# Key rows of every other group of four tokens built on ScalarE instead of VectorE, in a hybrid decoder step

## The reference, cut to what matters

```python
    e1 = jnp.take_along_axis(si[:, :, 0], ci // PEER_TOPK, axis=-1)
    e2 = jnp.take_along_axis(si[:, :, 1], ci % PEER_TOPK, axis=-1)
    experts = e1 * N_KEYS + e2
    g = jax.nn.softmax(cv, axis=-1)
    act = jax.nn.gelu(jnp.einsum('nhkd,nd->nhk', expert_u[experts], x).astype(jnp.float32))
    return jnp.einsum('nhk,nhkd->nd', (g * act).astype(x.dtype), expert_v[experts])
```

## Time and profile before

| | us |
|---|---|
| median of 3 runs | 2068.55 (2056.76 to 2073.18) |
| the profiled execution's own time | 2088.97 |
| its span | 2087.2 |
| PE busy | 1867.2 (89%) |
| DVE busy | 1522.3 (73%) |
| POOL busy | 654.2 (31%) |
| ACT busy | 608.7 (29%) |

### The profile page before, as it was taken

How to read it: one execution, slowest core, us unless ns; L and a number is a source line. 1 busy time by engine, 2 the same in 40 slices (tenths; PEclk the granted TensorE clock), 3 DMA queues, 4 the chain that set the end, 5 groups by cost and what they waited for, 6 DMA issues and landing times.

```text
span 2087.2 us, 26461 instructions
## 1 busy us (share of the span) xinstructions
PE 1867.2 (89%) x8833; PEld 1441.2 (69%) x8833; DVE 1522.3 (73%) x3495; ACT 608.7 (29%) x1037; POOL 654.2 (31%) x518
## 2 busy tenths in 40 slices
PE   6999899789997899699579789999999999999995
PEld 3556584366665664466457656888888888888884
DVE  4025238545546664679998878899999999999988
ACT  1133021200110120111245633443334343433343
POOL 0000001155635013414000012455555565566630
PEclk9989999866656558899789899999999999999998
DMA  6600335056647146656145589999999999999991
GB/s 258 234 32 33 112 122 191 15 152 211 223 157 261 56 138 225 242 202 244 59 152 203 230 315 328 333 392 381 388 397 389 379 381 386 398 381 384 383 340 43
DMA packets 157719, 508.71 MB, mean 244 GB/s; under 512 B 15760, under 2 KB 72640, under 8 KB 136128
## 3 DMA queue, kind: packets, MB, share of 16 engines
q1 hardware_dynamic: 90560, 266.44, 34.6%
q0 software_dynamic: 67072, 241.21, 31.1%
HBM read 474.69 MB, written 31.45 MB: 243 GB/s over the span
## 4 chain that ended last, share of the span: by engine, by line
PE 59%; DVE 22%; DMA 7%; issue 7%; ACT 3%; POOL 2%; SPq 0%; DVEq 0%; ACTq 0%
PE ps L1086 13%; PE ps L1070 12%; PE ps L677 5%; PE ps L1016 4%; DVE lo L2156 3%; PE ps L1032 2%; PE ps L825 2%; PE ps L786 2%; PE ps L1057 2%; DMA lo<-ur,lo 2%; PE ps L764 2%; PE ps L846 2%; PE ps L763 2%; PE ps L978 2%; POOL lo L1546 2%
## 5 line engine op out<-in xcount | busy, mean ns | idle before, releaser
L1546 POOL DMA_INDIRECT lo<-ur,lo x224 | 288.4, 1287 | 787.8 <-DVE lo L2093 345.0
L1546 POOL DMA_INDIRECT lo<-vr,lo x224 | 298.8, 1334 | 467.9 <-DVE lo L2164 300.2
L1086 PE MATMUL ps<-vh,hx 128*128 128x512 f32 x768 | 242.3, 397 | 23.6 <-DVE vl L2129 18.7
L1070 PE MATMUL ps<-xh,uh 128*128 128x320 f32 x832 | 257.8, 310 | 0.0
L1070 PE MATMUL ps<-xl,uh 128*128 128x320 f32 x832 | 257.1, 309 | 0.0
L1070 PE MATMUL ps<-xh,ul 128*128 128x320 f32 x832 | 256.8, 309 | 0.0
L1186 ACT ACTIVATE hi<-ps 128x512 f32<-128x512 f32 (+11 forms) x251 | 146.3, 626 | 326.4 <-PE ps L1016 107.7
L1086 PE MATMUL ps<-vl,hx 128*128 128x512 f32 (+1 forms) x768 | 240.4, 395 | 0.0
L2156 DVE SCALAR_TENSOR_TENSOR lo<-lo 128x1024 f32<-128x1024 f32 x168 | 215.4, 1282 | 11.8 <-DVE lo L2156 1.1
L1086 PEld LDWEIGHTS ps<-vh,hx 128*128 128x128 f32 x768 | 139.4, 189 | 60.1 <-issue 32.7
L2129 DVE TENSOR_TENSOR vl<-hi,vh 128x1024 fp32r<-128x1024 f32 x128 | 156.5, 1223 | 31.0 <-ACT vh L1186 14.3
(11 more groups left out here) (406 smaller groups left out, 3079.4 us busy)
## 6 DMA issues: line engine op xcount, KB each, us to landing
hi<-ev SPq DMA_DIRECT2D x64, 1024.0 KB
hi<-wts SPq DMA_DIRECT2D x22, 2048.0 KB, 7.5
hi<-eu SPq DMA_DIRECT2D x38, 1024.0 KB
lo<-eu SPq DMA_DIRECT2D x26, 1024.0 KB
gates<-hi SPq DMA_DIRECT2D x10, 2048.0 KB, 7.8
hi<-gates SPq DMA_DIRECT2D x30, 640.0 KB
lo<-cache SPq DMA_DIRECT2D x48, 128.0 KB
hi<-cache SPq DMA_DIRECT2D x48, 128.0 KB
```

What stands on the lines that cost most here:

```text
L1070: last = nc.tensor.matmul(ps[:, 6 + p, 0:GW[1]], a[p][:, k * 128:(k + 1) * 128], b[:, k, :], start=(k == 0 and b is xh and a is uh), stop= ...
L1086: last = nc.tensor.matmul(ps[m, 2 * slot(i) + half, :], a, b[p][:, half * 512:(half + 1) * 512], start=(first and n == 0), stop=(final and ...
L1546: nc.gpsimd.indirect_dma_start(ring[n % RING], None, table, bass.IndirectOffsetOnAxis(idxs[:, i, k:k + 1], 0)).then_inc(r_in[n % RING], 16)
```

## The change

For odd q, `oh1[q % 3]` is now made on ACT (`key_rows`): four activations, one for each token, write |key - column| (function Abs, the key as a per-partition bias), and after a wait for their completion a fifth writes max(0, 1 - that) over the four, in place: 1 where they are equal, 0 elsewhere. DVE makes `oh1` for even q alone, and `oh2` for all. PE waits for a second semaphore, `oh1_act`, in odd groups. ACT makes the rows of a tile's first odd group right behind the copy of `ohT`, and the rows of group q + 2 ahead of the copy of group q, for odd q.

```diff
--- before.py
+++ after.py
@@ -345,7 +345,7 @@
             "held_io pb_in idx_ready c_in0 c_in1 d_in0 d_in1 sm_s sm_max sm_mt sm_dg sm_mb sm_sub sm_exp sm_sum sm_o sm_div sm_t sm_done "
             "xm_ps xm_done wo_ps res_done pq_ps pq_done sc_ps sc_done tk_lin tk_exp tk_pick dup_in "
             "r_in0 r_in1 r_in2 r_in3 r_in4 r_in5 f_done dots_done gg_done "
-            "tr_ps tr_done oh1_done oh2_done gm_ps ev_done gs_in0 gs_in1 "
+            "tr_ps tr_done oh1_done oh1_act oh2_done gm_ps ev_done gs_in0 gs_in1 "
             "early_in0 early_in1 es_ps ea_done eo_out0 eo_out1 u_in0 u_in1 v_in0 v_in1 g_in0 g_in1 xh_done xl_done uh_done ul_done vh_done vl_done s_ps a_done hd_done hh_done hl_done "
             "y_ps yh_done acc_in out_tok out_state out_y").split()}
         w_in = [s["w_in0"], s["w_in1"]]
@@ -1049,7 +1049,7 @@
                         early_up(at, at + HS_TURN * KD)
                         at += HS_TURN * KD
                     for q in range((T[i] - S0) // 4, (T[i] - S0 + r) // 4):
-                        pe.wait_ge(s["oh1_done"], q + 1)
+                        pe.wait_ge(s["oh1_act" if q % 2 else "oh1_done"], q // 2 + 1)
                         pe.wait_ge(s["oh2_done"], q + 1)
                         if q >= 4:
                             pe.wait_ge(s["ev_done"], q - 3)
@@ -1388,6 +1388,15 @@
                     act.wait_ge(eo_out[b % 2], 16 * (b // 2))
                 nc.scalar.activation(ae[b % 2], ps[:, 5 + 2 * (b % 2), 0:GW[1]], ACT.Gelu_apprx_tanh).then_inc(s["ea_done"], 1)
 
+            def key_rows(i, q):
+                g = q - (T[i] - S0) // 4
+                if q >= 3:
+                    act.wait_ge(s["gm_ps"], q - 2)
+                for u in range(4):
+                    ins = nc.scalar.activation(oh1[q % 3][:, u, :], iota, ACT.Abs, bias=ohT[:, 0, 4 * g + u:4 * g + u + 1], scale=-1.0)
+                step(ins)
+                nc.scalar.activation(oh1[q % 3], oh1[q % 3], ACT.Relu, bias=1.0, scale=-1.0).then_inc(s["oh1_act"], 1)
+
             def gate_products():
                 for b in range(HS_GAP):
                     early_gelu(b)
@@ -1397,15 +1406,20 @@
                     r = R[i]
                     act.wait_ge(s["tr_ps"], slot(i) + 1)
                     if i > ST:
-                        act.wait_ge(s["oh1_done"], (T[i] - S0) // 4)
+                        act.wait_ge(s["oh1_done"], (T[i] - S0) // 8)
                         act.wait_ge(s["oh2_done"], (T[i] - S0) // 4)
                     copy(ohT[:, :, 0:r], ps[:, 6, 0:3 * r].rearrange("p (n t) -> p n t", n=3)).then_inc(s["tr_done"], 1)
                     if i == ST:
                         for b in range(HS_GAP, HS_GAP + HS_TURN):
                             early_gelu(b)
-                    for q in range((T[i] - S0) // 4, (T[i] - S0 + r) // 4):
+                    act.wait_ge(s["tr_done"], slot(i) + 1)
+                    q0, q1 = (T[i] - S0) // 4, (T[i] - S0 + r) // 4
+                    key_rows(i, q0 + 1)
+                    for q in range(q0, q1):
                         if q == (NCH - 1) * CH // 4:
                             round_v((0, 0), 16, None)
+                        if q % 2 and q + 2 < q1:
+                            key_rows(i, q + 2)
                         gates_copy(q)
                         for b in range(HS_GAP + HS_TURN, HS):
                             if EARLY_AT[b] == q:
@@ -2117,8 +2131,9 @@
                         dve.wait_ge(s["gm_ps"], q - 2)
                     v.tensor_tensor(oh2[q % 3].rearrange("p t (a b) -> p t a b", a=8), bc(high[:, 4 * g:4 * g + 4], 3, 16),
                                     bc(low[:, 4 * g:4 * g + 4], 2, 8), ALU.mult).then_inc(s["oh2_done"], 1)
-                    v.tensor_tensor(oh1[q % 3], bc(iota, 1, 4), bc(ohT[:, 0, 4 * g:4 * g + 4], 2, NK), ALU.is_equal)\
-                        .then_inc(s["oh1_done"], 1)
+                    if q % 2 == 0:
+                        v.tensor_tensor(oh1[q % 3], bc(iota, 1, 4), bc(ohT[:, 0, 4 * g:4 * g + 4], 2, NK), ALU.is_equal)\
+                            .then_inc(s["oh1_done"], 1)
 
             def low_u(p, n):
                 dve.wait_ge(s["uh_done"], n)
```

## The result

The changed kernel takes 2098.47 us (median of 4 runs, 2096.05 to 2102.96) against 2063.61 for the kernel before (4 runs beside it, 2056.76 to 2073.18): a ratio of 1.015, 95% interval 1.011 to 1.020. Forecast were 2095 and a range of 2072 to 2112. The profiled execution took 2098.93 us, its span is 2096.9.

The account below looks back on a forecast made before the run. The prediction took ScalarE's queue to become the bound in place of PE and VectorE. Its terms, 4.8 + 6.0 + 11.1 - 0.8 + 5.4 = 26.5, taken as +26 on the median 2068.55, gave 2095 us, range 2072 to 2112.

Parts of the forecast that it names:

- What bounds: In tiles 2 to 4, ScalarE's one queue becomes the bound: 3.7 us per pair of groups against 2.32; chance 0.54.
- The price of key rows: On ScalarE: four Abs 1.28 us, wait 0.05, fifth activation 0.625; next copy 1.86 after the start.
- tile 4: Q 48 to 63: copy 49 late by 1.4, seven pairs at 3.7 against 2.32 us; together +11.1 us.
- Tile 2: Q 0 to 15: PE's bursts wait for key rows, q 11 ends 5.4 late; +4.8 us after VectorE's saved comparison.
- Tile 3: Q 16 to 47: bursts of 7.9 us against 7.33 or 6.8; +10.8 at its end, 6.0 more than tile 2 left.
- rival 3: At chunk 7's store, the tail gives back up to 7.4 us of its 15.25: 2088 us; chance 0.12.
- chunk 8's key rows: Four more key rows, 7.4 us, free because ScalarE already waits 8.40 us for chunk 7's store.
- chunk 8's store: Starts later and shares less of the DMAs with chunk 7's store: 0 to -1.6 us, taken as -0.8.
- chunk 9's copies: The rows of q 75, 77 and 79 come between the eight copies: +5.4 us.
- Rival 1: VectorE's time comes back in tiles 2 and 3, key rows fit into gaps, tile 4 stays: 2054 us; chance 0.04.
- Rival 2: Tile 4 alone pays, tiles 2 and 3 break even, 15.7 us are left: 2084 us; chance 0.14.
- Rival 4: PE's clock falls in tile 4 (+4 us), with such stretches in tile 3 +7: 2102 us; chance 0.16.

Follow-up runs that it names:

- one_act: The changed kernel with key rows made by one activation of 512 columns, without the four Abs and their wait: 2063.59 us, ratio 1.000 to the kernel before.
- t23_only: Against the kernel before: ScalarE makes key rows for odd q of tiles 2 and 3 alone, tile 4 as before; 2083.41 us, ratio 1.008.
- t4_only: Against the kernel before: ScalarE makes key rows for odd q of tile 4 alone, tiles 2 and 3 as before; 2086.48 us, ratio 1.012.
- quarter_last: Against the kernel before: ScalarE makes key rows only for each burst's last group in tiles 2 and 3, in the change's place; 2080.04 us, ratio 1.007.

## Why the prediction was right, step by step

**What bounds.** As forecast: ScalarE's queue took the place of VectorE and PE, and its share of the page gave no hint of it.

**The price of key rows.** Four Abs 1.23 to 1.28 (1.28 forecast), Relu 0.63 (0.625), from the first Abs to the next copy 1.81 (1.86), two copies 1.75 (1.82), a pair 3.56 (3.7). The Relu starts 0.03 behind the end of the Abs, where 0.05 was taken. That made tile 4 cheaper than forecast: 9.9 instead of 11.1. The Trainium skill (ScalarE: Activation LUTs, What ACT_TABLE_LOAD costs) puts an activation with a per-partition bias at about 280 ns plus 0.833 a column, by which 128 columns are estimated at 387 ns. The trace agrees: the median of 160 is 387.

**Tile 2**, +5.3 for 4.8: held, with some luck. Q 12 starts 6.3 late where 5.4 were forecast, and 0.95 come back behind it where 0.6 were. The table load, in ScalarE's timeline:

```profile
1027.59 1.28 ACT L1370 ACT_TABLE_LOAD   x1
1028.88 0.31 ACT L1370 ACTIVATE hi<-hi 128x128 f32<-128x128 f32 x1
```

Here the input lay ready, and the exponential starts at the load's end. The drain of 1.38 us that the Trainium skill (ScalarE: Activation LUTs, What ACT_TABLE_LOAD costs) puts on top, and that the prediction left out, does not show: ScalarE's copy ends at 1027.57, 0.02 ahead of the load.

**Tile 3**, +10.9 for 6.0, is the term that was mis-sized, and the largest error. The mechanism was right, but its burst was too short, by 2.2 us over the tile; the comparison credited at q 16 made 1.0 and a clock dip 1.7. The chain of waits through one burst (start, us, what):

```profile
1107.83 1.08 ACT hi L1186
1108.91 1.04 ACT hi L1396 x4
...
1109.97 0.64 ACT hi L1398
...
1110.65 1.16 PE ps L1057 x8
1111.81 3.23 PE ps L1032 x12
```

I added 0.9 for the first product and 0.9 for its copy, which are distances between starts of neighbours. At a hand-over the next engine waits for the end. Product start to copy start is 1.09 (1114.88 to 1115.97), copy start to Abs 0.86, to the Relu's end 1.91, 0.05 to PE, 1.00 for the last product and 3.23 for `early_up`: 8.14, not 7.9. Against 7.33 that is +0.8 a burst, against 6.8 +1.35. The prediction's q 24 had +1.9 and shows +2.4. At q 16 it took off 0.7 for VectorE's comparison, and +0.26 was found. The clock dip is below.

**Chunk 7's store and rival 3.** SP issued it at 1181.53 and ScalarE went on at 1197.07:

```profile
1181.53 11.55 SPq L597 DMA_DIRECT2D gates<-hi  x2
...
1197.07 1.03 ACT L1186 ACTIVATE hi<-ps 128x512 f32<-128x512 f32 x1 [3.50 <-DMA gates<-hi]
```

15.5 us from issue, so nothing came back: rival 3 fell. ScalarE's wait shrank from 8.40 to 3.50, and chunk 8's key rows were covered, as forecast. The -0.8 for chunk 8's store was +0.2, and chunk 9's copies cost +4.85 for 5.4.

**Rival 1** (VectorE's time returns) fell: the 24 us became waiting for PE, and even one_act, whose key rows cost a third, gained nothing. **Rival 2** (tile 4 alone pays) fell by t23_only, +17. **Rival 4** (the clock) was right in the changed kernel's profile at one place and for 1.7 us only. A window of tile 3 behind q 27:

```profile
1087.00:1091.00 4.00, 4.00 (x12) 2.65 (x11) 3.90 (x6) 3.95 (x9) 0.00 (x0) 0.57 0.00 0
```

The granted clock was 0.57 there, near the lower of its two levels (1.2 GHz), and the 36 records of `early_up` took 11.55 us; in tile 2 they took 9.86. But in tile 4, for which the rival was written, with PE busy 18.8 of 30 us and idle for about 0.95 in every pair up to q 63, it was 1.00 (the second window at the top). In t4_only it did fall once behind q 63, to 0.62 from 1161 to 1164, and sixteen records took 3.26 us in place of 2.05. That cost nothing, since ScalarE set the pace: PE's next wait for it was 0.25 us in place of 1.5, and the pairs stayed 3.51 and 3.54 us apart. The swing that the Trainium skill names (TensorE: Matmul & The Clock Gate, A second HAM failure mode) so did not occur in that stretch of the changed kernel, and once in another execution of the same pattern.

The sum came out at 30.7 us against 26: tile 3 was 4.9 short, tile 2 0.5 short, tile 4 1.2 too long. By the medians the difference is 34.9, with an interval of about 22 to 40, so what lies above 30.7 can't be told from noise. That the time came within 3.5 us of the forecast is partly luck: the difference was 8.9 more than the 26 that were added, but the kernel before, measured beside the change, was 4.9 below the 2068.55 that they were added to. The prediction's own range has a slip: -0.35 on 20 key rows is 7 us, so its lower end is 2088, not 2084.

## What to carry to other kernels

An engine's spare time is counted in the stretch where work is to go, and at its place in that engine's queue: where key rows had to wait for a burst's first product, half of them cost nearly as much as all of them; behind a GELU that waited for PE a quarter of the groups cost 8 us, and one position earlier nothing. Where a chain passes from engine to engine, add durations to the end, not distances between starts. And before moving work, ask what the freed engine's time is worth: here, with VectorE's pace out of the way, three of tile 3's bursts fell only from 7.33 to PE's 6.80 us, and half or more of the 2.7 us won was gone before the loops.

## What the runs showed of the hardware

- The same idle time of PE left the clock alone at some places and not at others: in the changed kernel 2.82 us before 1031.07 in tile 2 did nothing (36 records in 9.86 us behind it), and 2.84 us before 1086.22 in tile 3 did (11.55, clock 0.57 from 1087 to 1091). With the same idle times it fell in tile 2 and not in tile 3 in t23_only (0.58 from 1031 to 1035, 1.00 from 1088 to 1092), and in both in quarter_last (0.50 from 1021 to 1023, 0.58 from 1079 to 1083). No run here tells what decides it, and each dip cost 1.5 to 1.7 us.
- ScalarE's wait for its own finished instruction costs 0.03 us (1158.97 behind 1157.70 + 1.24), so a step between dependent activations is nearly free; what costs is the queue behind it.
- A copy of 128x512 from PSUM that writes `stage` with a stride takes 1.03 to 1.10 us, the Relu of the same size from SBUF to SBUF 0.63. Why was not tried.
